# A hybrid decoder block: the up projection begins with the other half of the rows, combinations of h are made ahead, and low parts of w_up move from VectorE to GpSimd

## The reference

```python
x = x + rmsnorm(mix, g_post_mix[l])
h = rmsnorm(x, g_pre_mlp[l])
u = jnp.square(jax.nn.relu(jnp.einsum('bsd,df->bsf', h, w_up[l])))     # (2048, 1024) x (1024, 4096)
x = x + rmsnorm(jnp.einsum('bsf,fd->bsd', u, w_down[l]), g_post_mlp[l])
```

## Time and profile before

| | us |
|---|---|
| median of 3 runs | 2849.39 (2848.36 to 2851.91) |
| the profiled execution | 2846.14 |
| its span (first to last instruction) | 2844.4 |
| PE / DVE / ACT / POOL busy | 2735.8 / 1760.0 / 1345.0 / 671.0 |
| up projection, first matmul to down's first | 1567.7 to 2217.3 |

### The profile page before, as it was taken

The page is one execution under the profiler, slowest core; times in us unless marked ns, Lnnn a source line. Parts: engine busy times, 40 slices in busy tenths (PEclk is TensorE's granted clock), DMA queues, the critical chain, the costliest instruction groups (busy, mean ns, idle before and its releaser), DMA issues.

```text
span 2844.4 us, 36645 instructions
## 1 busy us (share of the span) xinstructions
PE 2735.8 (96%) x13362; PEld 2258.7 (79%) x13362; DVE 1760.0 (62%) x2456; ACT 1345.0 (47%) x2397; POOL 671.0 (24%) x577
## 2 busy tenths in 40 slices
PE   8999999999999999999999899979999999999997
PEld 6888888877787877887788688867888888888886
DVE  6211111179899899899645877787777545435566
ACT  5121111179788788788423544454444433322233
POOL 5220011036656557457212200010000000000013
PEclk9999999999999999999999999999999999999999
DMA  5443342463515414532464254433445556546577
GB/s 188 133 148 104 106 139 106 143 142 95 129 49 128 116 48 108 128 83 79 120 180 158 98 206 141 141 133 133 145 157 194 178 189 196 171 152 201 187 239 264
DMA packets 274410, 409.30 MB, mean 144 GB/s; under 512 B 18688, under 2 KB 133632, under 8 KB 274240
## 3 DMA queue, kind: packets, MB, share of 16 engines
q1 hardware_dynamic: 228416, 343.24, 39.6%
q10 hardware_dynamic: 45056, 63.05, 6.3%
q0 software_dynamic: 768, 0.79, 0.1%
HBM read 267.68 MB, written 139.33 MB: 143 GB/s over the span
## 4 chain that ended last, share of the span: by engine, by line
PE 62%; DVE 8%; ACT 4%; issue 4%; DMA 1%; POOL 0%; DVEq 0%; SPq 0%; ACTq 0%; POOLq 0%
PE ml_ps L2739 7%; PE ml_ps L2741 7%; PE ml_ps L2740 7%; PE ml_ps L2709 6%; PE ml_ps L2712 6%; PE ml_ps L2711 6%; PE at_ps_t L1486 5%; PE at_ps_s L1462 3%; PE at_ps_s L1468 3%; PE mo_acc L1803 2%; PE mo_acc L1805 2%; PE mo_acc L1804 2%; ACT at_probs L1313 2%; PE at_ps_o L1501 2%; PE at_ps_o L1502 2%
## 5 line engine op out<-in xcount | busy, mean ns | idle before, releaser
L2709 PE MATMUL ml_ps<-ml_h_hiM,ml_w_hi 128*128 128x512 f32 x896 | 352.8, 394 | 29.1 <-ACT ml_t L2434 12.6
L1361 DVE TENSOR_REDUCE at_nmax<-at_ps_s 128x1 f32<-128x1024 f32 (+7 forms) x384 | 347.0, 907 | 37.6 <-PE at_ps_s L1468 35.3
L2711 PE MATMUL ml_ps<-ml_h_loM,ml_w_hi 128*128 128x512 f32 x896 | 351.6, 392 | 0.0
L2712 PE MATMUL ml_ps<-ml_h_hiM,ml_w_lo 128*128 128x512 f32 x896 | 351.2, 392 | 0.0
L2739 PE MATMUL ml_ps<-ml_b_hi,ml_a_hi 128*128 128x512 f32 x896 | 348.7, 389 | 1.3 <-DVE ml_a_lo L2226 1.3
L2740 PE MATMUL ml_ps<-ml_b_lo,ml_a_hi 128*128 128x512 f32 x896 | 348.6, 389 | 0.0
L2741 PE MATMUL ml_ps<-ml_b_hi,ml_a_lo 128*128 128x512 f32 x896 | 348.5, 389 | 0.0
L598 DVE SCALAR_TENSOR_TENSOR pj_out_sb<-pj_acc,pj_out_sb 128x512 fp32r<-128x512 f32 x96 | 66.4, 692 | 424.1 <-ACT pj_out_sb L534 424.1
L1370 DVE TENSOR_TENSOR at_p_lo<-at_ps_t,at_p_hi 128x512 fp32r<-128x512 f32 x480 | 280.2, 605 | 35.8 <-ACT at_p_hi L1331 32.9
L1331 ACT ACTIVATE at_p_hi<-at_ps_t 128x512 fp32r<-128x512 f32 x480 | 249.2, 534 | 86.9 <-PE at_ps_t L1486 48.0
L1486 PE MATMUL at_ps_t<-at_ident_r,at_probs 128*128 128x128 f32 x1632 | 249.7, 275 | 15.0 <-DVE at_p_lo L1370 8.2
(11 more groups left out here) (263 smaller groups left out, 6025.9 us busy)
## 6 DMA issues: line engine op xcount, KB each, us to landing
ml_a_raw<-ua SPq DMA_DIRECT2D x112, 512.0 KB, 4.0
qk<-pj_out_sb ACTq DMA_DIRECT2D x64, 512.0 KB, 2.8
ml_w_raw<-in_w_up_dram SPq DMA_DIRECT2D x64, 512.0 KB, 4.8
ua<-ml_t SPq DMA_DIRECT2D x128, 256.0 KB, 2.5
ml_b_raw<-in_w_down_dram SPq DMA_DIRECT2D x56, 512.0 KB, 5.0
at_q<-qk SPq DMA_DIRECT2D x96, 256.0 KB
at_k<-qk SPq DMA_DIRECT2D x96, 256.0 KB
ua<-ml_x SPq DMA_DIRECT2D x96, 256.0 KB, 2.4
```

What stands on the lines that cost most here:

```text
L1361: dve.tensor_reduce(nmax[:, par, sc.a, s, sc.part:sc.part + 1], ps_s[:, sc.g % 2, 0:sc.width], AX.X, ALU.max, negate=True).then_inc(maxed, 1)
L2709: pe.matmul(to, hi, h_hi[m][:, k, :], start=begins and k == 0, stop=False, skip_group_check=not begins)
L2711: pe.matmul(to, hi, h_lo[m][:, k, :], start=False, stop=False, skip_group_check=not begins)
L2712: last = pe.matmul(to, lo, h_hi[m][:, k, :], start=False, stop=k == 3, skip_group_check=not begins)
```

## The change

- The early half of the rows is now the first sweep: tiles 0 to 7 stay in `h_rows`, tiles 8 to 15 go to DRAM through one buffer, and the output tiles follow.
- The right sides of M1, M6 and M7 are made in 12 pieces of 128x512 (sum, high, low), stored to a new DRAM tensor `hc`, and fetched when their place is free. For the first sweep that is done in the mixing stage (tiles 9 to 13), for the second in units 1 to 6, two pieces a unit, through the ring `x`. The sums of M4 and M3 are made in place in `h_rows`. All low parts of h are now DVE's, whole.
- `lo_w` runs on POOL from step 3 on; steps 0 to 2 are DVE's.
- The last flip of the mixing stage stands behind both halves of M4 instead of one.
- The rows of x2 at the end have four buffers.

The core of the diff:

```diff
     def lo_w(eng, step):
-        if step >= 7 * UN:
-            return
         eng.wait_ge(w_hi_ready, step + 1)
-        if step < 3:
-            wait_ring(eng, step)
-        if step == 2:
-            eng.wait_ge(w_ready, 2)
+        if step in (1, 2):
+            eng.wait_ge(mix.y_step, 2 * (RT - 3 + step) + 2)
...
+    HI_H = {(TOP, 1): "M2", (TOP, 2): "M4", (TOP, 5): "M3", (TOP, 6): "M5"}
+    LO_H = {(TOP, 2): "M2", (TOP, 4): "M4", (TOP, 6): "M3", (UC, 1): "M5"}
+
+    def staged_at(n):
+        return (2 * n - 2, 2 * n - 1) if 1 <= n <= len(pieces) // 2 else ()
...
+    def wait_rows(eng, sweep):
+
+        if sweep:
+            eng.wait_ge(h_loaded, 16 * KT)
+        else:
+            eng.wait_ge(mix.h_ready, RT // 2 + 2)
...
+    def sum_piece(dve, sweep, n):
+        m, k = pieces[n]
+        op, one, two = RIGHT[m]
+        wait_rows(dve, sweep)
...
+    def sum_in_place(dve, sweep, m):
+        op, one, two = RIGHT[m]
+        wait_rows(dve, sweep)
+        dve.tensor_tensor(h_quarter(one), h_quarter(one), h_quarter(two), op).then_inc(h_summed, 1)
...
+    def fetch_h(sp, sweep, m):
+        n = STAGED.index(m)
...
+        for z, tile in enumerate((h_hi[m], h_lo[m])):
+            sp.dma_start(f32(tile[:, :, :]), hc[sweep, n, z].rearrange("k p n -> p k n")).then_inc(h_fetched[n], 16)
...
     @block.gpsimd
     def _(pool):
...
+        mix.gpsimd(pool)
+        pool.wait_ge(w_ready, 3)
+        for step in range(3, 7 * UN):
+            lo_w(pool, step)
...
     @block.vector
     def _(dve):
+        def first(dve, t):
+            if t == RT - 1:
+                lo_w(dve, 1)
+
         def within(dve, t):
-            if t == RT - 5:
+            if RT - 7 <= t < RT - 3:
+                for n in range(3 * (t - RT + 7), 3 * (t - RT + 7) + 3):
+                    sum_piece(dve, 0, n)
+            if RT - 6 <= t < RT - 2:
+                for n in range(3 * (t - RT + 6), 3 * (t - RT + 6) + 3):
+                    lo_piece(dve, 0, n)
+            if t == RT - 4:
                 sum_w(dve, 0)
             if t == RT - 3:
-                sum_h(dve, 0, "M4", WHOLE)
+                sum_in_place(dve, 0, "M4")
+                sum_in_place(dve, 0, "M3")
             if t == RT - 2:
-                lo_h_dve(dve, 0, "M2", WHOLE)
-                lo_h_dve(dve, 0, "M4", WHOLE)
+                lo_h(dve, 0, "M2")
+                lo_h(dve, 0, "M4")
+                lo_w(dve, 0)
             if t == RT - 1:
-                sum_h(dve, 0, "M3", BEGIN)
+                lo_h(dve, 0, "M3")
+                lo_w(dve, 2)
...
         for n in range(UN):
             for i in range(7):
-                if n or i:
-                    lo_w(dve, 7 * n + i + 1)
+                if (n, i) == (0, 0):
+                    lo_h(dve, 0, "M5")
                 sum_w(dve, 7 * n + i + 2)
                 if i == 0 and n:
                     combine_late(n - 1)
...
+                if (n, i) in LO_H:
+                    lo_h(dve, 1, LO_H[n, i])
+                if staged_at(n) and i in (3, 5):
+                    lo_piece(dve, 1, staged_at(n)[(i - 3) // 2])
+                if staged_at(n) and i in (2, 3):
+                    sum_piece(dve, 1, staged_at(n)[i - 2])
+                if n == UC - 1 and i in (0, 1):
+                    sum_in_place(dve, 1, IN_PLACE[i])
```

More of the change, by code:

```diff
@@ L1627, in scale @@
                                ALU.pow).then_inc(rstd_step, 1)
-        with pool.Fori(0, LAST) as t:
+        with pool.Fori(0, RT) as t:
             for n in range(2):
                 scale(t, n)
[L1632 to L1636, removed]
     def split_hi(act, k):
@@ L1890, in mlp @@
     gain = place("gain", high(88), [P, D])
-    xres = [place(f"xres{s}", high(92 + 4 * s), [P, D]) for s in range(2)]
+    xres = [place(f"xres{s}", high(at), [P, D]) for s, at in enumerate((92, 96, 114, 118))]
     rows_out = [place(f"rows_out{s}", high(100 + 4 * s), [P, D]) for s in range(3)]
@@ new lines, in wait_staged @@
+    def wait_staged(eng):
+        for s in range(3):
+            eng.wait_ge(x_stored[s], FIRST_STAGE)
+    def sum_piece(dve, sweep, n):
+        m, k = pieces[n]
+        op, one, two = RIGHT[m]
+        wait_rows(dve, sweep)
+        if sweep == 0:
+            to = stage_sum[n % 6]
+            if n >= 6:
+                dve.wait_ge(x_stored[n % 3], 32 * (n // 3 - 1))
+        else:
+            slot, turn = x_use["piece", n, "sum"]
+            to = x_ring[slot]
+            dve.wait_ge(x_stored[slot], FIRST_STAGE + 16 * turn)
+        dve.tensor_tensor(to[:, :], h_quarter(one)[:, k, :], h_quarter(two)[:, k, :], op).then_inc(h_summed, 1)
@@ new lines, in hi_piece, with lo_piece @@
+    def hi_piece(act, sweep, n):
+        act.wait_ge(h_summed, h_sum_no[sweep, pieces[n]])
+        if sweep == 0:
+            of, to = stage_sum[n % 6], stage_hi[n % 6]
+        else:
+            slot, turn = x_use["piece", n, "hi"]
+            of, to = x_ring[x_use["piece", n, "sum"][0]], x_split[slot]
+            act.wait_ge(x_stored[slot], FIRST_STAGE + 16 * turn)
+        act.activation(to[:, :], of[:, :], ACT.Copy).then_inc(h_hi_ready, 1)
+    def lo_piece(dve, sweep, n):
+        if sweep == 0:
+            of, to, hi = stage_sum[n % 6], stage_lo[n % 6], stage_hi[n % 6]
+        else:
+            slot = x_use["piece", n, "sum"][0]
+            of, to, hi = x_ring[slot], x_split[slot], x_split[x_use["piece", n, "hi"][0]]
+        dve.wait_ge(h_hi_ready, h_split_no[sweep, pieces[n]])
+        dve.tensor_tensor(to[:, :], of[:, :], f32(hi[:, :]), ALU.subtract).then_inc(h_lo_ready, 1)
@@ new lines, in store_piece @@
+    def store_piece(sp, sweep, n):
+        m, k = pieces[n]
+        if sweep == 0:
+            parts = (stage_hi[n % 6], n % 3), (stage_lo[n % 6], n % 3)
+        else:
+            parts = ((x_split[x_use["piece", n, z][0]], x_use["piece", n, z][0]) for z in ("hi", "sum"))
+        sp.wait_ge(h_lo_ready, h_split_no[sweep, pieces[n]])
+        for z, (tile, slot) in enumerate(parts):
+            sp.dma_start(hc[sweep, STAGED.index(m), z, k], f32(tile[:, :])).then_inc(x_stored[slot], 16)
+    def sum_in_place(dve, sweep, m):
+        op, one, two = RIGHT[m]
+        wait_rows(dve, sweep)
+        dve.tensor_tensor(h_quarter(one), h_quarter(one), h_quarter(two), op).then_inc(h_summed, 1)
@@ new lines, in hi_h, with lo_h @@
+    def hi_h(act, sweep, m):
+        op, one, _ = RIGHT[m]
+        if op is None:
+            wait_rows(act, sweep)
+        else:
+            act.wait_ge(h_summed, h_sum_no[sweep, m])
+        if sweep:
+            act.wait_ge(done, 2 * (7 * (UC - 1) + NO[m] + 1))
+        elif m in ("M2", "M4"):
+            wait_staged(act)
+        else:
+            act.wait_ge(mix.multiplied, TOGETHER)
+        act.activation(h_hi[m][:, :, :], h_quarter(one), ACT.Copy).then_inc(h_hi_ready, 1)
+    def lo_h(dve, sweep, m):
+        dve.wait_ge(h_hi_ready, h_split_no[sweep, m])
+        dve.tensor_tensor(h_lo[m][:, :, :], h_quarter(RIGHT[m][1]), f32(h_hi[m][:, :, :]), ALU.subtract)\
+           .then_inc(h_lo_ready, 1)
@@ L2374, in _ @@
             if step == LATE:
-                load_x(0)
-                load_x(1)
+                for no in range(4):
+                    load_x(no)
             for no in range(len(outs)):
```

358 lines of the change are left out of this document (157 added, 201 removed).

## The result

The changed kernel took 2828.28 us (median of 4 runs, 2826.93 to 2829.86), and the kernel before, run beside it, 2848.88 (4 runs, 2845.56 to 2851.91). The ratio is 0.9928 (95%: 0.9911 to 0.9945): faster, by 20.6 us or 0.7%. The prediction was 2827.4, in a range of 2814 to 2846.

A forecast was written before the change was run, and what follows sets the result against it. TensorE, busy 96% of the span, was taken as the bound, with 38.7 us lost to waits and low clock in up. Terms 15.2 + 14.8 + 3.5 - 2.2 - 9.3 = 22.0 us off gave median 2827.4, range 2814 to 2846.

The forecast's parts named there:

- start of up: Units 0 and 1 of up: first products need only early rows, 1.6 us lost instead of 16.8; gain 15.2 us.
- mixing stage: Tiles 9 to 14: added VectorE work mostly hidden, tiles 12 and 13 late; loss 2.2 us, bounds 0 and 8.
- new wait of unit 1: M5 of unit 1 waits for eight loads of h: stall 7.1, clock 2.2; loss 9.3 us.
- low parts, steady units: 109 low parts of w moved from VectorE to GpSimd, sharing a port: cost 0 in steady units.
- change of sweeps: Units 7 and 8 of up: less work there, 7.1 us lost instead of 21.9; gain 14.8 us.
- tail: End of kernel: four buffers for x2 close gaps before VectorE's last final steps; gain 3.5 us, bounds 0 and 4.5.
- the walk: The prediction's step-by-step engine timing; tile 12's flip 0.4 us late, tile 13's flip 0.8 and split 1.0 more.
- Rival C: Port blocking delays ACT's take of M2 at unit edges; slower if 1.6 us lost in each of 14 units; chance 0.08.
- the slower rival: Same as Rival C: the shared port makes the kernel slower, 2861 us with 2.4 us lost per unit; chance 0.08.
- A: Unit 1: loads of h early enough or VectorE late enough, new wait costs nothing; 2818 us; chance 0.12.
- D: Losses only move among mixing, new wait and change of sweeps, sum unchanged; 2845 to 2852 us; chance 0.09.
- B: Start and change of sweeps: gains real but half, VectorE late and blocked; 2838 us; chance 0.21.

The follow-up runs named there:

- e3: Changed kernel with two buffers for the rows of x2 instead of four; one execution: 626.4 us from down's first matmul to the span's end, against 623.9.
- e8: Kernel before with one part of the change alone, low parts of w by GpSimd from step 3 on; median 2853.5 us, ratio 1.0025.
- e10: Changed kernel, but the two loads of h that unit 1's pieces need are issued first and waited for alone; median 2824.7 us, ratio 0.9918.
- e7: Changed kernel, but all eight loads of the second half of h are issued in unit 0, not unit 1; median 2831.1 us, ratio 0.9942.
- e2: Changed kernel, but all low parts of w are made by VectorE again, none by GpSimd; median 2823.3 us, ratio 0.9919.
- e12: Changed kernel with e10's edit and M2's low part of h behind unit 7's take of M3, GpSimd keeping w's low parts; median 2817.0 us, ratio 0.9898.
- e1: Changed kernel, but unit 1's first two pieces are made behind VectorE's takes of M3 and M5, not ahead; median 2828.6 us, ratio 0.993.

## Why the prediction was right, term by term

| term | forecast | measured | read from |
|---|---|---|---|
| start of up | +15.2 | +13.3 | loss at M4 of unit 1: 17.4 and 4.1 |
| mixing stage | -2.2 | -1.8 | 175.4 and 177.2 |
| new wait of unit 1 | -9.3 | -10.3 | 4.1 to 14.4 |
| low parts, steady units | 0 | 0 | units 2 to 6 and 9 to 15 |
| change of sweeps | +14.8 | +13.5 | 22.0 and 8.5 behind unit 2 |
| tail | +3.5 | +3.2 | 627.1 and 623.9; 2.4 by the means with e3 |
| sum | +22.0 | +17.9 | profiled executions: 18.2 |

The 0.3 us between the last two numbers lie between the mixing stage's last product and the first of up, which follows 1.0 us later and not 1.4. The medians lie 20.6 apart and the forecast median was 0.9 off, but that closeness is luck: the forecast of the profiled execution, 2824.1, was 3.9 too low, and the one before had happened to be 3.3 under its median, this one only 0.3. The two large gains, start and change, are read from the waits that went, at the places forecast; e8 shows that the low parts did not bring them. No run has the other half of the rows, the pieces made ahead or the last flip alone, so how the gains divide among these is not shown.

**Mixing stage.** The rows of tiles 12 and 13 delay the next product by 0.4 and 1.5 us, where the walk had 0.4 and 1.8.

**Start.** 1.6 us were to be lost. It is 1.9 in unit 0 (2.7 less the flip's 0.8), and the take of M2 in unit 1 adds 1.4, which the walk did not have: POOL's low part falls among the combinations of unit 0, and ACT's take of M2 comes late. The two rows of the changed kernel (DVE's three take 1.9 us where nothing holds them up):

```profile
1607.12 5.16 DVE L2623 TENSOR_TENSOR ml_x<-ml_t,ml_t 128x512 f32<-128x512 f32 x3 [1.17 <-ACT ml_t L2463]
```

```profile
1609.24 2.49 POOL L2111 TENSOR_TENSOR ml_w_lo<-ml_w_raw,ml_w_hi 128x1024 fp32r<-128x1024 f32 x1 [0.92 <-ACT ml_w_hi L2105]
```

The prediction gave 1.1 us of slack for exactly this take and let it be enough everywhere.

**New wait.** Right in place and cause: stall 7.4 (7.1 forecast), clock and the rest 2.9 (2.2). That the stall's size came out is luck in part. The loads landed 23.8 us into the unit (22.0 forecast), since SP issued them 11.0 us into it (8.8 forecast), and PE was itself later at M5, at 17.8 (16.3); the two errors cancel. That the stall is the landing of rows is shown by e10, and e7 shows that issuing all of them earlier only moves it. I had not seen that one line of wait, for eight loads where two are read, was all of it.

**Low parts.** The steady units cost nothing, as forecast. But the cost was looked for only there. e2, e8 and e12 put it at 7.7, 3.7 and 5.1 us in up, at the edges and the change of sweeps, where DVE is full. A part of it was in the forecast's 3.9 us at unit 7. Rival C had the mechanism and asked for 14 places. ACT's late take of M2 costs in three (M4 of units 1, 7 and 8: 1.4, 0.9, 1.0), and only in the first two is some of it POOL's doing: with DVE's low parts it is 0.6, nothing and 0.9 (e2). So C did not decide the sign. "DVE 100 us less" was wrong: it is 51 (497.9 to 446.4 in 650 us), since a blocked instruction counts as busy. POOL's 109 low parts took 272.5 us, not 262. The Trainium skill's sentence that such offloading "might not help" (Perfetto Trace Analysis, Optimizing Scalar/DVE Operations), put down to the slower rival, was right about this part, and the gains of the others hid it.

**Change of sweeps.** M5 of unit 7 waits 4.6 (3.9 forecast) and the clock takes 2.2 (1.5); the takes of M2 cost 0.9 and 1.0 in units 7 and 8 (1.1 was said of unit 8, nothing of unit 7), and the take of M3 in unit 8 costs 0.1 to 0.2 (0.6 was said). The mechanism was right; what was short is the wait of unit 7 with its clock, and M2's take there. The three terms that were short, start, new wait and change, all ran against the kernel: 4.2 us in the profiled execution.

**Rivals.** A (no new wait) and D (losses only move) fall by the table; B's half gains too, since 13.3 and 13.5 came of 15.2 and 14.8.

## What to carry to other kernels

When an instruction in an in-order row waits for loads, wait for those it reads and issue them first; moving the instruction or the whole burst moved most or all of the stall elsewhere here (e1, e7), and splitting the wait took it away (e10). Before giving work from VectorE to GpSimd, walk the places where VectorE's row is full: an idle engine's 2.4 us hold up just the instructions that are late there. A gain of many parts should be taken apart again afterwards, since one of them may be a loss.
